# The down projection with tokens as rows, and it and half of the convolution's out-projection by seven products of sums

## The reference

```python
def conv_mixers(h, w_in, w_out, a_dw_w, a_dw_b, a_ln_g, a_ln_b, b_dw_w):
    z = h @ w_in
    a_val, a_gate, b_gate, c_gate, b_val = jnp.split(z, CONV_SPLITS, axis=-1)
    ya = a_val * jax.nn.sigmoid(a_gate)
    ya = depthwise_conv(ya, a_dw_w) + a_dw_b
    ya = jax.nn.silu(layer_norm(ya, a_ln_g, a_ln_b))
    yb = b_gate * depthwise_conv(c_gate * b_val, b_dw_w)
    return jnp.concatenate([ya, yb], axis=-1) @ w_out          # 1024 x 1024
...
# first network, layer 0 (256 tokens of x and 256 of ctx): convolution mixer, norm, experts
x_lat = layer_norm(DEEPNORM_ALPHA * x_lat + g1 * y_lat, ln1_g[i], ln1_b[i])
...
# second network, one layer (256 tokens)
merged = jax.nn.sigmoid(ga) * y_ssm + jax.nn.sigmoid(gb) * y_att
h = h + gate1 * (merged @ w_out[layer])
u2 = rms_norm_2(h, norm2_g[layer]) * (1.0 + scale2) + shift2
ffn = (jax.nn.silu(u2 @ w_ffn_gate[layer]) * (u2 @ w_ffn_up[layer])) @ w_ffn_down[layer]
h = h + gate2 * ffn                                            # FFN_HIDDEN = 2816
return rms_norm_2(h, final_g)
```

## Time and profile before

| | before |
|---|---|
| time, median of 3 runs | 1971.03 us (1969.43 to 1973.2) |
| the profiled execution's own time | 1968.86 us |
| its span, first to last instruction | 1966.8 us |
| PE busy | 1757.7 us (89%) |
| DVE busy | 1028.2 us (52%) |
| ACT busy | 414.4 us (21%) |
| mean granted TensorE clock | 0.955 |

### The profile page before, as it was taken

The page is one execution under the profiler, slowest core; times in us unless marked ns, Lnnn a source line. Parts: engine busy times, 40 slices in busy tenths (PEclk is TensorE's granted clock), DMA queues, the critical chain, the costliest instruction groups (busy, mean ns, idle before and its releaser), DMA issues.

```text
span 1966.8 us, 56056 instructions
## 1 busy us (share of the span) xinstructions
PE 1757.7 (89%) x23585; PEld 1214.4 (62%) x23586; DVE 1028.2 (52%) x2435; ACT 414.4 (21%) x826; POOL 559.9 (28%) x423
## 2 busy tenths in 40 slices
PE   6999989999999997998988976666667999999998
PEld 4544466666666664645676754444445787888887
DVE  3898156767666766775444543233237996210001
ACT  2001242211221113204441211111113314210001
POOL 0000026767777762001026832222225000100000
PEclk9999989999999999999999988888888999999999
DMA  9854168999999999924269999999999433333320
GB/s 364 324 217 171 43 252 332 430 428 429 411 430 414 428 429 401 362 105 161 86 247 429 411 429 428 429 428 428 429 428 350 137 120 129 129 129 128 136 99 22
DMA packets 109376, 574.28 MB, mean 292 GB/s; under 512 B 4976, under 2 KB 10224, under 8 KB 84592
## 3 DMA queue, kind: packets, MB, share of 16 engines
q1 hardware_dynamic: 108720, 570.72, 72.4%
q10 hardware_dynamic: 576, 2.43, 0.3%
HBM read 572.08 MB, written 1.05 MB: 291 GB/s over the span
## 4 chain that ended last, share of the span: by engine, by line
PE 67%; DMA 25%; DVE 3%; ACT 2%; SPq 2%; issue 1%; DVEq 0%; ACTq 0%
PE bank L372 28%; DMA ring<-in_expert_w_up 17%; PE bank L587 15%; DMA ring<-in_expert_w_down 7%; PE bank L559 4%; PE bank L1051 4%; PE bank L537 3%; PE bank L634 2%; ACT b L1952 2%; PE bank L444 1%; PE bank L965 1%; DMA ring<-in_conv_w_in 1%; PE bank L398 1%; SPq L2475 1%; PE bank L756 1%
## 5 line engine op out<-in xcount | busy, mean ns | idle before, releaser
L587 PE MATMUL bank<-ring,b 128*32 128x128 f32 (+1 forms) x13600 | 520.5, 310 | 130.2 <-DMA ring<-in_expert_w_gate 69.5
L587 PEld LDWEIGHTS bank<-ring,b 128*32 128x32 f32 x13600 | 402.3, 116 | 302.2 <-issue 154.3
L1111 DVE TENSOR_TENSOR h_t<-h_t,bank 128x512 f32<-128x512 f32 (+1 forms) x696 | 349.7, 564 | 306.8 <-PE bank L559 306.8
L372 PE MATMUL bank<-h_t,ring 128*128 128x256 f32 (+1 forms) x1600 | 427.3, 429 | 8.4 <-ACT h_t L1952 5.9
L1952 ACT ACTIVATE b<-bank 128x256 f32<-128x256 f32 (+5 forms) x362 | 140.8, 406 | 1224.2 <-PE bank L587 741.5
L372 PEld LDWEIGHTS bank<-h_t,ring 128*128 128x128 f32 x1600 | 308.6, 194 | 120.5 <-issue 80.1
L2418 POOL TENSOR_SCALAR b<-b 128x1024 f32<-128x1024 f32 (+1 forms) x85 | 195.3, 2298 | 53.8 <-POOL b L2426 29.7
L2426 POOL TENSOR_TENSOR b<-b 128x512 f32<-128x512 f32 (+1 forms) x85 | 89.1, 1049 | 377.0 <-PE bank L559 376.5
L559 PE MATMUL bank<-b 32*128 32x512 f32 (+1 forms) x1392 | 170.2, 559 | 5.7 <-DVE h_t L1111 4.7
L1111 DVE TENSOR_TENSOR b<-b,bank 128x128 f32<-128x128 f32 (+3 forms) x124 | 49.9, 407 | 237.0 <-PE bank L372 154.1
L2421 POOL TENSOR_TENSOR b<-b,b 128x1024 f32<-128x1024 f32 (+1 forms) x85 | 161.7, 1902 | 7.1
(11 more groups left out here) (325 smaller groups left out, 1420.5 us busy)
## 6 DMA issues: line engine op xcount, KB each, us to landing
ring<-in_expert_w_gate SPq DMA_DIRECT2D x64, 2048.0 KB, 18.5
ring<-in_expert_w_up SPq DMA_DIRECT2D x64, 2048.0 KB, 20.7
ring<-in_expert_w_down SPq DMA_DIRECT2D x64, 2048.0 KB, 20.9
ring<-in_ada_w SPq DMA_DIRECT2D x24, 2048.0 KB, 14.2
ring<-in_w_mod SPq DMA_DIRECT2D x12, 2048.0 KB, 20.1
ring<-in_w_in SPq DMA_DIRECT2D x6, 2048.0 KB, 14.3
ring<-in_w_ffn_gate SPq DMA_DIRECT2D x5, 2048.0 KB, 7.9
ring<-in_w_ffn_up SPq DMA_DIRECT2D x5, 2048.0 KB, 7.8
```

The lines of the kernel that those rows point to most:

```text
L372: last = pe.matmul(o, lhs(k), rhs(k), start=(k == 0), stop=(k == nk - 1))
L587: last = pe.matmul(b[32 * m:32 * m + 32, 0:width], lhs[:, k, :], rhs[:, k, m * width:(m + 1) * width], start=(k == 0), stop=(k == nk - 1), ...
L1111: return dv.tensor_tensor(o, a, b, op)
```

## The change

The two products are computed in another way: both operands are cut in two along both sides, and the four quarters of the result are sums of seven products of sums of quarters, in place of eight products of quarters. With A cut into a11, a12, a21, a22 and B likewise, s1 = a21 + a22, s2 = s1 - a11, s3 = a11 - a21, s4 = a12 - s2, t1 = b12 - b11, t2 = b22 - t1, t3 = b22 - b12, t4 = b21 - t2, and the products are a11 b11, a12 b21, s4 b22, a22 t4, s1 t1, s2 t2 and s3 t3 (numbers 1 to 7).

- In the second chunk of the convolution's out-projection A is the weights and B the tokens. PE makes seven groups of 2 x 4 products of 128 x 256 in lane "v". DVE makes the eight sums, scales the upper half of `X` by ALPHA ahead of time, and adds each group straight to the quarters of `X` to which it belongs (28 instructions at L1596 of the new file, each with the gate in it). ACT gates only the first chunk.
- In the down projection A is the hidden values, with tokens as rows, and B the weights: per chunk of four blocks, seven products of two instructions with 512 moving columns, into seven banks that sum over all chunks. DVE makes four sums of the hidden values per chunk during the gate and up projections, and four sums of the weights per chunk, the first chunk's before the down projection and the others' beside it, a chunk ahead.
- The result then has tokens as rows. So `X2` is turned by 16 transposes in the up projection of the first piece, and the gate and the final gain, which lie along the channels, are needed as rows that are equal in all partitions: PE turns them once, DVE spreads them over a diagonal (`row_blocks`), four products by ones with 512 moving columns make the rows (`spread_row`), and ACT takes them into `gate_row` and `gain_row`.
- The end: DVE and, for one quarter, GpSimd (POOL) combine the seven banks into the four quarters of the residual, ACT squares and sums along the row, and ACT and DVE scale the rows into `fin`. `turn_rows`, `mean_square` and the steps at L1930 and L1933 are gone.

```diff
+        out_order = (1, 2, 6, 5, 7, 3, 4)
@@ PE, convolution
-            channel_out(n + 1, "a", lambda k: conv_y[:, k, :], KD, 512, TOK)
+            loaded(n + 1)
+
+            def out_product(i):
+                (a11, a12), (s3, a22) = out_weights(n + 1)
+                (b11, _), (b21, b22) = out_tokens
+                s1, s2, s4, t1, t2, t3, t4 = out_sums
+                lhs, rhs = {1: (a11, b11), 2: (a12, b21), 3: (s4, b22), 4: (a22, t4), 5: (s1, t1), 6: (s2, t2), 7: (s3, t3)}[i]
+
+                def emit(b):
+                    for m in range(2):
+                        last = sum_k(b[:, SEQ * m:SEQ * m + SEQ], lambda k: lhs[:, k, m * P:(m + 1) * P], lambda k: rhs[:, k, :], 4)
+                    return last
+                group("v", emit)
+
+            for i in out_order:
+                if i == 6:
+                    pe.wait_ge(sem("out_sums"), 8)
+                out_product(i)
@@ PE, around rms2 and the gate and up projections
+            def spread_row(v, h):
+                group("a", lambda b: pe.matmul(halves(b), ones_c[0:32, :], row_blocks[:, 4 * v + 2 * h:4 * v + 2 * h + 2, :],
+                                               start=True, stop=True))
+            pe.wait_ge(v_free, marks["row_blocks"][0])
+            for h in range(2):
+                spread_row(0, h)
             spread_inverse("rms2", SEQ)
+            for h in range(2):
+                spread_row(1, h)
...
+                if j == 0:
+                    for t in range(2):
+                        for h in range(2):
+                            group("v", lambda b: transposes(b, [(P * i, X2[:, 4 * h + i, t * P:(t + 1) * P]) for i in range(4)]))
@@ PE, down projection
-            def down(m, k, wt):
-                return pe.matmul(bank[m][:, 0:SEQ], wt[:, k % 4, m * P:(m + 1) * P], f_hid[:, k, :],
-                                 start=(k == 0), stop=(k == KF - 1))
+            def product(i, c):
+                (a11, a12), (_, a22) = hidden(c)
+                s3 = hidden(c)[1][0]
+                s1, s2, s4 = hidden_sums(c)
+                (b11, t3), (b21, b22) = down_weights(c)[1]
+                t1, t2, t4 = weight_sums(c)
+                lhs, rhs = {1: (a11, b11), 2: (a12, b21), 3: (s4, b22), 4: (a22, t4), 5: (s1, t1), 6: (s2, t2), 7: (s3, t3)}[i]
+                h = down_half(c)
+                for kk in range(h):
+                    last = pe.matmul(bank[i - 1][:, :], lhs[:, kk, :], rhs[:, kk, :],
+                                     start=(c == 0 and kk == 0), stop=(c == 5 and kk == h - 1))
+                return last
             for c in range(4):
+                loaded(down_weights(c)[0])
+                for i in (1, 2):
+                    product(i, c)
+                pe.wait_ge(sem("hidden_sums"), 4 * c + 4)
+                pe.wait_ge(sem("weight_sums"), 4 * c + 4)
+                for i in (4, 6, 5, 7, 3):
+                    last = product(i, c)
+                last.then_inc(sem("down_step"), 1)
+            for c in (4, 5):
+                loaded(down_weights(c)[0])
+            for i in (1, 2, 6, 5, 7, 3, 4):
+                if i == 6:
+                    pe.wait_ge(sem("hidden_sums"), 24)
+                    pe.wait_ge(sem("weight_sums"), 24)
+                product(i, 4)
+                product(i, 5).then_inc(sem("product_full"), 1)
@@ DVE
+            def sum_weights(c):
+                n, ((b11, b12_), (b21, b22)) = down_weights(c)
+                t1, t2, t4 = weight_sums(c)
+                dv.wait_ge(slot_loaded[n % RING], 16 * loads_until(n))
+                if c > 1:
+                    dv.wait_ge(sem("down_step"), c - 1)
+                weight_sum(tt(t1, b12_, b11, ALU.subtract))
...
+                if m % 4 == 3 or m == KF - 1:
+                    sum_hidden(m // 4)
+                if m == 19:
+                    sum_weights(0)
+            for c in range(1, 6):
+                sum_weights(c)
...
+            made(7)
+            do(tt(u3, prod[4], gate[0], ALU.mult))
+            tt(x_rows(1, 0), u3, r21, ALU.add).then_inc(sem("final_rows"), 1)
             dv.wait_ge(sem("rms3_root"), 2)
+            dv.reciprocal(st[:, 8:10], st[:, 16:18]).then_inc(sem("rms3_inverse"), 1)
...
+                dv.scalar_tensor_tensor(halves(fin[:, t, 0:512]), x_rows(t, 0), st[:, 8 + t:9 + t], fg[0], ALU.mult, ALU.mult) \
@@ POOL
+            po.wait_ge(sem("final_rows"), ends["y22"])
+            do(po.tensor_tensor(y22, y22, gate[1], ALU.mult))
+            po.tensor_tensor(x_rows(1, 1), x_rows(1, 1), y22, ALU.add).then_inc(sem("pool_rows"), 1)
```

More of the change, by code:

```diff
@@ L331, in made_by, with loads_until @@
             return [(a, k + 1)] + ([(v, k - 1)] if k >= 2 else [])
+        left_out = [start["after"] + j for j, c in enumerate(after) if c is None]
+        def loads_until(n):
+            return n // RING + 1 - sum(m < n and m % RING == n % RING for m in left_out)
         block = ctx.enter_context(nc.Block())
@@ L1032, in _ @@
             channel_out(n + 15, "v", lambda k: atto[:, k, :], 4, 1024, SEQ)
+            pe.wait_ge(sem("row_sources"), 1)
+            group("v", lambda b: transposes(b, [(0, row_src)]))
+            mark("row_blocks")
             n += 6
@@ new lines, in _ @@
+            tt(x_rows(0, 0), x_rows(0, 0), y11, ALU.add).then_inc(sem("final_rows"), 1)
+            made(3)
+            do(tt(u2, z1, prod[6], ALU.add))
+            made(4)
+            do(tt(u4, u2, prod[5], ALU.add))
+            do(tt(r12, u4, gate[1], ALU.mult))
+            do(tt(r12, r12, x_rows(0, 1), ALU.add))
+            made(5)
+            step(tt(u3, u2, prod[7], ALU.add))
+            tt(y22, u4, prod[7], ALU.add).then_inc(sem("final_rows"), 1)
+            done()
+            do(tt(u3, u3, gate[0], ALU.mult))
@@ L2174, in _ @@
             fetch_root()
-            gated(0, 2, TOK, H)
+            gated(0, 2, TOK, H, range(4))
             norm_stats(0, TOK)
```

215 lines of the change are left out of this document (157 added, 58 removed).

## The result

| | before | changed |
|---|---|---|
| time, median | 1971.1 us (4 executions, 1969.43 to 1973.2) | 1954.21 us (4 executions, 1953.53 to 1954.49) |
| the profiled execution's own time | 1968.86 us | 1954.33 us |
| its span | 1966.8 us | 1952.3 us |
| mean granted TensorE clock | 0.955 | 0.960 |

The ratio of changed to before is 0.9929, 95% interval 0.9904 to 0.9955. A second comparison on another chip gave 1949.98 us for 1966.09, 0.9927 (0.991 to 0.9945). So by the ratio the change saves about 14 us, with an interval from 9 to 19; the two medians are 16.9 us apart, the two profiled executions 14.5. The forecast was 1954.7 us.

What follows compares the result with a forecast made beforehand. PE, busy 89% of the span, was taken to bound the kernel. Terms -3.1 - 0.4 + 1.1 + 2.1 - 11.9 - 1.1 - 3.0 sum to -16.3 us, giving 1954.7 us against the median; range 1951.0 to 1960.0.

Steps and rivals of the forecast that it cites:

- convolution's products: Convolution's out-projection, second chunk: 112 records of 256 columns in 24.34 us for 27.47, -3.1 us; bound -3.4.
- gate projection later: Before the gate projection: the products making gate and gain rows start it 1.1 us later, bounds 0 and +1.7.
- transposes, gate and up at full clock: Up projection: sixteen transposes and one of small rows, +2.1 us; clock kept from the rows into the gate projection, -3.0 us.
- down products: Down projection: 154 records of 512 columns take 66.1 us for 78.02, -11.9 us, with no wait for DVE.
- the end: From the last down product to the span's end: 7.9 us for 8.96, -1.1 us (-1.3 to +1).
- the terms from rms2 on (B): From rms2's first sum to the end of the span: rows, transposes, clock, down projection and end, -12.8 us forecast.
- What this stage saves is passed on whole: Convolution's out-projection: its saving reaches the end through the experts' stage, as nothing from outside sets the clock there.
- the case that they let it down: Up projection: transposes might lower the clock, costing 3.4 us, about 1958 us; part of the clock-falls rival, chance 0.22.
- the threshold of 12.0 us for a chunk's sums: Down projection: DVE's weight sums hold PE up only if a chunk's take over 12.0 us; about 1975 us, slower 0.03.
- GpSimd's quarter ... 0.5 us before the last product ends: The end: two GpSimd steps of 1.29 us and ACT's square of 0.62 finish 0.5 us before the last product.
- I expect the clock to stay at 2.4 GHz: -3.0 us: From the gate rows into the gate projection: with PE's idle time filled, the clock does not fall, -3.0 us; chance 0.60.
- 0.22 for the fall: Behind the rows made with 32 partitions: rival that the clock falls all the same, 1957.7 us, chance 0.22.

Runs made afterwards that it cites:

- the second of the kernels with blocks at the end: Changed kernel plus 11 PE-only stretches behind its end, each ten full products then a block of 32-output, 32-row, full products or transposes: 2142.44 us, one execution.
- The convolution alone: The kernel before with only the convolution's part of the change: 1963.64 us against 1965.34, ratio 0.999.
- The two halves: The kernel before with only the convolution's part, ratio 0.999; the changed kernel with the convolution as before, 1958.96 us, ratio 0.9967.
- the changed kernel with full rows: Changed kernel with the four products that make gate and gain rows over all 128 partitions, zeros in the other 96: 1953.67 us, ratio 0.9942.

## Why the prediction was right, and where it wasn't

The forecast was 1954.7 us against the median, and 1952.6 against the profiled execution; measured were 1954.21 and 1954.33.

| term | forecast | clock fell (changed) | clock kept (the same kernel again) |
|---|---|---|---|
| convolution's products | -3.1 | -3.30 | -3.30 |
| its end | -0.4 | -0.2 | -0.2 |
| gate projection later | +1.1 | +1.90 | +0.89 |
| transposes, gate and up at full clock | +2.1, -3.0 | +1.03 | -1.30 |
| down products | -11.9 | -11.66 | -11.66 |
| the end | -1.1 | -0.53 | -0.53 |
| the terms from rms2 on (B) | -12.8 | -9.25 | -12.59 |

**Convolution.** Right: 112 records of 256 columns at 0.2158 us, nearer the bound of half of 512 columns (-3.4). DVE had its sums ready at 213.2 us, earlier than the 215.5 worked out; the norm's sums take 0.2 and not 0.4 us less. "What this stage saves is passed on whole" is shown for the stage, and for the span as far as the spread lets one see: from the convolution's first chunk to rms2's first sum it is 1509.70 and 1509.64 us in the two executions without the change to the convolution, and 1503.1 to 1507.9 in 11 of the 12 with it; the twelfth, the second of the kernels with blocks at the end, had 1510.5. The experts' first load inside the loop comes 99.72 and 101.51 us after L765 without the change, and 95.2 to 98.5 in all 12 with it.

**Rows.** +1.1 was forecast, +0.89 with the clock kept: right. In the execution shown the gain rows ran at half clock, which makes +1.90.

**Transposes.** Sixteen take 1.75 us, 0.109 each, where 0.125 each and one more made 2.1. Back to back 56 took 6.12 us, and the clock stayed at 1.00 through three such blocks, so the case that they let it down has fallen. The Trainium skill ("TensorE: Matmul & The Clock Gate", Part 4: PE-mode transpose) gives about 275 ns for one and says that it doesn't count as activity in the same way. A record of these transposes lasts 272 ns, so the figure agrees as a duration; as a price in a row of them it is more than double, since one starts every 0.109 us. The clock of 1.00 through three blocks doesn't fit the second statement, and the measurement decides here.

**Down projection.** Right to 0.2 us, and by the mechanism given: no wait for DVE between chunks, 2.3 us of slack in the last (2.2 worked out), and the threshold of 12.0 us for a chunk's sums is bracketed by doubling and trebling them.

**The end.** The step that failed in size is "GpSimd's quarter ... 0.5 us before the last product ends". Two steps of 1.29 us were taken from a row of another stage. They took 1.65 and 1.60, and the quarter's last one ended at 1941.90 + 1.61 = 1943.51 us, 0.3 before the last product's end, with ACT's square still to come; one sum of DVE took 1.64 and not 0.69. The square and its sum ended at 1943.54 + 0.73 = 1944.27, DVE's small step on the mean (L2106) waited for it, and so DVE took up the last product at 1944.36, 0.5 us after its end: -0.53 for -1.1.

```profile
1940.74 1.64 DVE L1181 TENSOR_TENSOR b<-b,x_t 128x512 f32<-128x512 f32 x1
...
1944.29 0.15 DVE L2106 TENSOR_SCALAR sm<-sm 128x1 f32<-128x1 f32 x1 [0.24 <-ACT b L2134]
1944.36 0.68 DVE L1181 TENSOR_TENSOR b<-bank,b 128x512 f32<-128x512 f32 x1
```

A step of POOL that the last square waits for was one of the prediction's own signs of being wrong, and so was a clock of 0.50 behind the rows; both came.

**The clock.** "I expect the clock to stay at 2.4 GHz: -3.0 us" was inferred from PE's idle time, and idle time is not what decided. PE was busy but for 0.1 us from rms2's first sum to the fall, and in four of the eight profiled executions the clock fell. The price is right: 3.34 us between two executions of one kernel. The chance was not: 0.22 for the fall, where half of them had it. (The last chances also miss the cases that they come from by 0.01: 0.94 and 0.03, not 0.95 and 0.02.) That the time still met the forecast so closely is in part luck. In the profiled execution the terms of the sum came to -12.7 us, the transpose of the small rows included, and not to -16.3; 1.0 us at the start and 0.9 between the norm's sums and rms2, in parts that the change doesn't touch, gave back 1.9. The median met it with two medians that are 16.9 us apart, where the ratios of both comparisons give about 14.

**What stays open.** The convolution alone showed 1.7 us where its stage gained 3.3. The two halves make 8.1, the changed kernel with full rows 11.7 on the same chip; the intervals (about 3 us to either side of each half, 4 of the whole) allow both. Against about 14 us on other chips the gap is 6 us, at the edge of the intervals; another explanation wasn't shown. What in an execution decides whether the clock falls behind the rows is open too: nothing in the kernel differed, and the kernel before, without the rows, had it fallen in both of its profiled executions of this stage (the second is the convolution alone). The Trainium skill ("TensorE: Matmul & The Clock Gate", Part 1: The HAM clock gate) says that the same kernel shows a different number of slow products from run to run, as the monitor doesn't start with the kernel. It says so of the slow products at a kernel's start. It would fit here too, but no run here can show when the monitor looks.

## What to carry to other kernels

Where PE alone sets the end, seven products for eight are worth nearly their full eighth, less what the operands' other layout costs (2.6 us of rows and transposes here), as long as another engine's sums per chunk take less time than PE's products per chunk, the shorter last chunk on its own. Filling a gap of PE with work doesn't by itself keep the clock: products over all rows held it in both executions that had them there, those over 32 rows in half. Small products packed into different groups of rows cost less time; whether they hold the clock isn't shown. Before a step of GpSimd is put beside DVE at the end of a kernel, price both at their slowed durations, and take one profiled execution for one sample of the clock, not for the kernel's.

## What the hardware showed that I had not expected

- Products with 32 of 128 rows, 16 records in a row with PE always busy, brought the granted clock to 0.63 to 0.75 over the block and 0.76 to 0.87 over the full products behind it, in seven of seven blocks; products with 32 of 128 output channels left it at 1.00 in seven of seven.
- Three products with 32 rows each, in three different groups of rows, took 1.13 us; two in the same group, four records, 1.77.
- DVE and GpSimd slow each other, and the one that starts second pays: 1.20 to 1.64 us for 0.69 in a DVE sum of two SBUF tiles of 128 x 512, 1.59 to 1.75 for 1.27 in a step of GpSimd.
- One kernel's time varies by 11.8 us between executions on one chip (1960.51 to 1972.29 in 27 executions of the kernel before). In the changed kernel the clock behind rms2 alone made 3.3 us between two profiled executions.
